# Splitting weights on GpSimd piece by piece in a two-layer hybrid encoder

## The reference

```python
def _hybrid_layer(x, ...):
    h = _rms_norm(x, norm_mix)
    z = jnp.einsum('bsd,de->bse', h, w_in)                  # 1024 -> 6340 columns
    za, bq, bk, bv, cq, clat, ciq, cik, ciw, zd, zg = _split(z, IN_SIZES)
    ya = _gmlp_mixer(jax.nn.gelu(za), ...)                  # chunked spatial gating
    yb = _swa_sink_mixer(bq, bk, bv, ...)                   # sliding-window attention with sinks
    yc = _dsa_mixer(cq, clat, ciq, cik, ciw, ...)           # indexer, top 64 keys, attention
    yd = _pool_mixer(zd, ...)                               # causal pooling
    gates = jax.nn.sigmoid(zg).reshape(Bsz, S, N_BRANCH, D_MODEL)
    merged = (gates[:, :, 0] * (ya @ a_w_out) + gates[:, :, 1] * (yb @ b_w_out)
              + gates[:, :, 2] * (yc @ c_w_out) + gates[:, :, 3] * (yd @ d_w_out))
    x = x + merged @ w_o
    h2 = _rms_norm(x, norm_ffn)
    gate, up = jnp.split(h2 @ w_gate_up, 2, axis=-1)        # 1024 -> 2 x 2816
    return x + (jax.nn.silu(gate) * up) @ w_down
```

## Time and profile before

| what | value |
|---|---|
| median of three executions | 906.06 us (903.81 to 906.17) |
| profiled execution, first to last instruction (its span) | 902.6 us |
| TensorE busy | 835.4 us, 93% |
| VectorE busy | 591.8 us, 66% |
| ScalarE busy | 410.8 us, 46% |
| GpSimd busy | 185.4 us, 21%, of it splits 147.1 us in 36 instructions |

### The profile page before, as it was taken

The page is one execution under the profiler, slowest core; times in us unless marked ns, Lnnn a source line. Parts: engine busy times, 40 slices in busy tenths (PEclk is TensorE's granted clock), DMA queues, the critical chain, the costliest instruction groups (busy, mean ns, idle before and its releaser), DMA issues.

```text
span 902.6 us, 11887 instructions
## 1 busy us (share of the span) xinstructions
PE 835.4 (93%) x3876; PEld 678.3 (75%) x3876; DVE 591.8 (66%) x827; ACT 410.8 (46%) x559; POOL 185.4 (21%) x116
## 2 busy tenths in 40 slices
PE   4997979699989999999979979887999899999998
PEld 3886757578868888888868867665788688888886
DVE  8799487976646646546378975788846565645643
ACT  4755245363535444444356634353543444443440
POOL 6244212624220000000024422423431200000000
PEclk8999889799999999999999979998999999999999
DMA  6743234354554656555654515252543556556641
GB/s 205 260 128 130 94 117 139 119 175 161 178 153 147 213 175 199 186 183 190 175 177 131 183 60 187 93 168 77 177 147 134 187 186 197 192 172 199 193 168 47
DMA packets 99091, 144.43 MB, mean 160 GB/s; under 512 B 11728, under 2 KB 62416, under 8 KB 99024
## 3 DMA queue, kind: packets, MB, share of 16 engines
q1 hardware_dynamic: 99024, 143.60, 49.2%
HBM read 142.54 MB, written 1.05 MB: 159 GB/s over the span
## 4 chain that ended last, share of the span: by engine, by line
PE 74%; DVE 10%; issue 8%; DMA 3%; ACT 3%; SPq 2%; DVEq 0%; ACTq 0%
PE big L1382 14%; PE big L1386 14%; PE big L1385 14%; PE mix L1382 9%; PE mix L1386 9%; PE mix L1385 9%; DVE w_lo L957 2%; DMA w_raw<-in_w_in 2%; DVE act_lo L974 1%; ACT w_hi L625 1%; SPq L538 1%; PE mix L1660 1%; DMA w_raw<-in_w_gate_up 1%; DVE row L1118 1%; DVE row L1121 1%
## 5 line engine op out<-in xcount | busy, mean ns | idle before, releaser
L625 ACT ACTIVATE w_hi<-w_raw 128x2048 fp32r<-128x2048 f32 (+2 forms) x140 | 256.2, 1835 | 168.4 <-DMA w_raw<-in_w_gate_up 108.3
L957 DVE TENSOR_TENSOR w_lo<-w_raw,w_hi 128x2048 fp32r<-128x2048 f32 (+2 forms) x108 | 242.9, 2264 | 42.5 <-ACT w_hi L625 42.0
L595 POOL TENSOR_TENSOR w_lo<-w_raw,w_hi 128x2048 fp32r<-128x2048 f32 (+2 forms) x36 | 147.1, 4096 | 441.8 <-ACT w_hi L625 441.8
L1382 PE MATMUL big<-w_hi,act_hi 128*128 128x512 f32 (+2 forms) x480 | 193.1, 402 | 18.8 <-DVE act_lo L974 10.0
L1385 PE MATMUL big<-w_lo,act_hi 128*128 128x512 f32 (+2 forms) x480 | 187.2, 390 | 0.0
L1386 PE MATMUL big<-w_hi,act_lo 128*128 128x512 f32 (+2 forms) x480 | 186.8, 389 | 0.0
L1382 PE MATMUL mix<-w_hi,act_hi 128*128 128x512 f32 x352 | 138.6, 394 | 7.6 <-DVE act_lo L974 7.6
L1386 PE MATMUL mix<-w_hi,act_lo 128*128 128x512 f32 x352 | 138.5, 394 | 0.0
L1385 PE MATMUL mix<-w_lo,act_hi 128*128 128x512 f32 x352 | 138.4, 393 | 0.0
L1382 PEld LDWEIGHTS big<-w_hi,act_hi 128*128 128x128 f32 x480 | 93.3, 194 | 44.0 <-issue 12.9
L1386 PEld LDWEIGHTS big<-w_hi,act_lo 128*128 128x128 f32 x480 | 92.8, 193 | 18.3
(11 more groups left out here) (189 smaller groups left out, 848.8 us busy)
## 6 DMA issues: line engine op xcount, KB each, us to landing
w_raw<-in_w_in SPq DMA_DIRECT2D x44, 1024.0 KB, 5.1
w_raw<-in_w_gate_up SPq DMA_DIRECT2D x88, 512.0 KB, 4.7
w_raw<-in_w_down SPq DMA_DIRECT2D x22, 1024.0 KB, 4.9
w_raw<-in_w_o SPq DMA_DIRECT2D x8, 1024.0 KB, 5.0
w_raw<-in_b_w_out SPq DMA_DIRECT2D x4, 1024.0 KB, 5.0
w_raw<-in_w_in SPq DMA_DIRECT2D x4, 904.0 KB, 6.3
w_raw<-in_w_in SPq DMA_DIRECT2D x4, 512.0 KB, 3.5
w_raw<-in_a_w_out SPq DMA_DIRECT2D x4, 512.0 KB, 4.0
```

Of the source, the lines that this page charges most:

```text
L595: nc.gpsimd.tensor_tensor(low(u)[:, a:b], arrived(u)[:, a:b], high(u)[:, a:b].bitcast(F32), ALU.subtract).then_inc(lo_by_pool.sem, 1)
L625: nc.scalar.activation(high(u), arrived(u), ACT.Copy).then_inc(hi_ready.sem, 1)
L957: nc.vector.tensor_tensor(low(u)[:, a:], arrived(u)[:, a:], high(u)[:, a:].bitcast(F32), ALU.subtract).then_inc(lo_by_dve.sem, 1)
L1382: ins = nc.tensor.matmul(dst[:, 0:w], xh, wh, start=first and n == 0, stop=False)
```

## The change

In GpSimd's `split`, each group of pieces that was one subtraction is issued as one subtraction for each piece. The wait ahead of the group and the single increment of the semaphore behind it stay; the increment now stands on the last piece's operation. Nothing else is touched, on GpSimd or on another engine.

```diff
                 pool.wait_ge(*hi_ready.nth(l, u + 1))
                 for a, b in ((0, 2), (2, 4)) if u == 0 else ((0, 2),) if u == SHARED else ((0, unit_pieces(u)),):
-                    nc.gpsimd.tensor_tensor(low(u)[:, a:b], arrived(u)[:, a:b], high(u)[:, a:b].bitcast(F32),
-                                            ALU.subtract
-                                            ).then_inc(lo_by_pool.sem, 1)
+                    for piece in range(a, b):
+                        ins = nc.gpsimd.tensor_tensor(low(u)[:, piece], arrived(u)[:, piece],
+                                                      high(u)[:, piece].bitcast(F32), ALU.subtract)
+                    ins.then_inc(lo_by_pool.sem, 1)
```

## The result

The changed kernel takes 867.5 us, the median of four executions (865.46 to 870.05), against 904.93 us for the kernel before (four executions, 898.15 to 906.17). The ratio is 0.961, 95% interval 0.957 to 0.965.

A forecast was written before the change was run, and what follows sets the result against it. TensorE's halts (67 us) were put down to VectorE instructions waiting for GpSimd's splits to end. Gains of 9.75 us in the first layer and 11.45 in the second, together 21.2, took 906.06 to 885 us, range 870 to 899.

The forecast's parts named there:

- units 23 to 25: Merges ahead of TensorE's transposes: shorter waits were to gain 5.9 us in layer 1 and 5.4 in layer 2.
- the longer unit 11: Unit 11 ends later in pieces: TensorE waits about 1 us, taken up by its halt before the spatial matmul.
- Price of a piece: GpSimd's time for a 512-column piece: 1.35 us, with bounds 1.12 and 1.49; 0.31 us of it fixed.
- The dense stretch: VectorE's instructions up to the spatial matmul, units 9, 11 and 13: a net loss of 1.2 us in each layer.
- At unit 13: End of VectorE's stretch before the spatial matmul: its last L1089 ends at 91.15 instead of 91.60, a gain of 0.45 us.
- the terms of units 16, 18 and L1070: VectorE waits between spatial matmul and merges, first layer: −0.7 us at unit 16, +1.55 at unit 18, +0.45 at L1070.
- unit 38: Split before the feed-forward part: its second half was to start at 269.15 instead of 272.90, +3.75 us in each layer.
- The lower bound of a piece: A quarter of the 4.49 us for 2048 columns, 1.12 us for a piece; it gave 876 us in all.
- rival 2: VectorE wins every seam between GpSimd instructions, some 10 us more gain per layer: 865 us, 11 in 100.
- Rival 1: No turns inside a unit: VectorE waits the whole 5.4 us instead of 4.49; slower, 922 us, 7 in 100.
- Rival 3: Another wait closes TensorE's holes, for weights or ScalarE's place in its queue; half the gain, 895 us, 14 in 100.
- Rival 4: Nothing moves, since the stalls only change their place: 906 us, 5 in 100.

The follow-up runs named there:

- the kernel with units 9, 11 and 13 alone: Only units 9, 11 and 13 of each layer issued piece by piece, other units whole as in the kernel before; 899.72 us, ratio 0.995.
- the kernel with unit 38 alone: Only unit 38 of each layer issued piece by piece, the others whole as in the kernel before; 891.92 us, ratio 0.986.
- units 16 and 18 alone: Only units 16 and 18 of each layer issued piece by piece, the others whole as in the kernel before; 900.46 us, ratio 0.995.

## Why the prediction was right in direction and wrong in size

**Right: who waits for whom.** VectorE instructions with two operands in SBUF wait for the end of a GpSimd instruction, and at each end the engines change over, inside a unit too. L1140 takes 1.58 us beside pieces for 4.87 before, L958 3.36 for 6.66, L975 1.38 for 4.64; none of them lasts over 2.1 us except L958, whose own work is 2.28. The Trainium skill (SBUF — State Buffer, Who interferes with whom) has the same rule, a pair of ports that one instruction holds until its end; the three durations of one merge, 4.48, 2.18 and 1.06 us, agree with it. The page has the order of issue decide who blocks; it does not say which engine follows when each has an instruction waiting. That they alternate is what the timelines show. Right too were the places, the order of their sizes (units 23 to 25 first, then 38), that the lead is kept to the end, and that the longer unit 11 costs TensorE little: 0.21 us for the 1 us estimated. The "some 30" of 36 splits at which the pattern was to repeat is too many; I count 23 that hold a VectorE instruction for more than 0.7 us.

**Wrong: the price of a turn, the step "Price of a piece" and all that is counted with it.** The prediction charged 1.35 us for a piece and then VectorE's instruction in full, 2.0 us for a piece and a merge. The measured turn is 1.70 us. Of the 0.30 us, 0.10 is the piece itself, which starts 1.25 us after the one before it where nothing stands between. The other 0.2 us is the changeover: a piece and the merge, 1.25 and 0.69 us one after the other, make 1.94 and take 1.70. The merge costs GpSimd 0.45 us and not the 0.65 charged. Half of this stood in the earlier trace rows: the split of 162.06, with one merge ahead of it, lasts 5.03 us for 4.49, which is 0.54. Why it is 0.45 stays open. That each hides some of the other's fixed part is my reading; that it needs the next piece to stand in line is ruled out by the wait between pieces, which leaves the turn at 1.71. It changes these terms:
- Units 23 to 25: four merges with their pieces were to take from 157.50 to 165.5, 8.0 us; they take from 153.03 to 159.96, 6.9. From the first split to the transposes the prediction has 12.5 us, the trace 163.84 − 153.03 = 10.8, and before it was 18.4. The gain is 7.6 us for 5.9.
- The dense stretch: unit 11 was to block VectorE for 5.03 us and blocks it for 4.0, unit 9 for 2.95 and blocks it for 1.9; as one operation they cost 4.3 and 2.0. So the many short turns win a little where they were to lose 1.65 us. At unit 13, L1090 ends 1.3 us sooner where 0.45 was predicted. The halt at the spatial matmul shrinks by 2.5 us in each layer, where it was to grow by 1 us. This step had the wrong sign, and with 2.7 and 3.6 us of halts won for −1.2 and −0.4 it makes 7.9 of the 9.8 us that the forecast missed in halts.

In between, up to the first merge of unit 23, the terms of units 16, 18 and L1070 were +1.3 us together. That merge starts 158.17 − 153.73 = 4.4 us sooner, of which 1.7 were there at the spatial matmul, so 2.7 were won.

**Wrong: the clock was left out.** The prediction read, in its first paragraph, that a spell at the lower clock follows each halt, and then gave it no term. (Each is too much: before, the granted clock is 1.00 from 458 to 475, behind a halt of 2.54 us and two of 1.08 and 1.41.) TensorE's busy time fell by 7.8 us with the halts. At unit 38 that is 1.2 us between the two halves. Another 1.5 us lie between the transposes and the halt for act_lo: the same 408 matmuls, with no halt among them, are busy for 88.06 us at a granted clock of 0.98 before, and for 86.5 at 1.00 after. Not all stretches win by it: up to the spatial matmul of the first layer TensorE's busy time grew by 1.1 us, while the halt shrank. Of the 17.7 us that the forecast missed, 7.8 are this term. About 10 are left, all of them halts, and I put them down to the turns: the kernel with units 9, 11 and 13 alone shows it for the dense stretch, the rows of the merges for units 23 to 25. At unit 38 it is the whole miss, since the halts there gave 3.1 and 2.9 us for the 3.75 predicted.

**The bounds.** The lower bound of a piece, 1.12 us, gave 876, and rival 2 was to cover what lay below. The bounds took a piece's price alone and added VectorE's time in full in every case, so they did not hold the cost of a turn; and they had nothing for the clock.

**The rivals.** Rival 1, no turns inside a unit, falls: no VectorE instruction beside the pieces waits longer than one piece, and the wait added between pieces only costs. Rival 2, VectorE wins every seam, falls as well, though its 865 us are nearest to the result: L1033, L1034 and L1035 follow one another from 69.66 on, each reads two operands from SBUF, and each waits for a piece of its own (1.41, 1.51 and 1.67 us, for 0.43, 0.42 and 0.69 alone). Had VectorE won every seam, the second and third would have run at once. That a wrong mechanism gave the nearer number is a coincidence of sizes. Rival 3 falls: it named a load or ScalarE as what TensorE would wait for, and no halt over 0.3 us has one of them as releaser that had not before. The new waits, 1.2 us in all at 512 columns, are for GpSimd's own units; they set the limit at 128. Rival 4 falls.

**What stays open.** Why a merge costs GpSimd 0.45 us. Why three executions of the kernel with unit 38 alone were 4 to 6 us faster than the traced one, whose gain is the expected one. And why units 16 and 18 alone gain 4.6 us in the median, although their profile shows the later halts partly filled up again. The last is near the spread between executions.

## What to carry to other kernels

Where VectorE and GpSimd both read two operands from SBUF, look at the same VectorE instruction with and without a GpSimd instruction beside it; if it has two durations, the length of GpSimd's instructions is a latency in VectorE's queue, and cutting them is worth trying even though GpSimd's busy time grows (here by 18%, its waits for VectorE among it, for 4% less time). Cut until the engine behind begins to wait for GpSimd: here 256 columns, where an operation takes 0.70 us of which some 0.14 is fixed. When a halt of TensorE goes, count the slower matmuls behind it as well, and measure a changeover between two engines as a whole instead of adding the two instructions.

## What the runs showed of the hardware

- Alone on GpSimd, subtractions of 1024, 512, 256 and 128 columns start 2.37, 1.25, 0.70 and 0.42 us apart, and one of 2048 lasts 4.49: about 0.14 us fixed and 2.1 ns for a column (0.14 + 2048 × 0.00212 = 4.48; 0.14 + 128 × 0.00212 = 0.41). The 0.31 us that the prediction drew from rows of 1024 and 2048 columns is more than double that: a row's duration holds some 0.05 us of overlap with the next, and two long rows measure a small constant badly.
- A merge of 0.69 us between two GpSimd operations moves the second by about 0.45 us at every length: 2.82 us from start to start for 2.37, 1.70 for 1.25, 1.15 for 0.70, 0.87 to 0.9 for 0.42. So the changeover has a price that does not depend on the operation cut.
- L1157, with one operand in PSUM, runs in 0.67 us beside the pieces and does not wait, so it fills the time in which L1165 could not run anyway.
- The kernel before spreads more than the ones with short operations: its executions took 898 to 906 us, those with 256 columns 854.1 to 855.5. Why is not shown.
